# Cross attention: the softmax of the prompt's heads ahead of one weight split on two in-order engines

## The chip, the cores and the metric

The kernel runs on one core of a Trainium2 chip. The metric is the device time of one execution in microseconds; three runs of the kernel before gave 1637.77, 1638.6 and 1644.74, median 1638.6.

## The reference

A two-layer trunk in float32 over 256 prompt tokens and 8 x 4 decoding tokens (288 columns), width 1024. Each layer has a gated feed-forward block, a mixing block (convolution, dilated attention, a linear recurrence), a cross attention, and a second feed-forward block. What the change touches is the cross attention. The prompt's keys and values come from a memory of 256 tokens, the decoding tokens' from caches:

```python
def cross_attend(h, mk, mv, w_q, w_o):
    B, T, D = h.shape
    q = (h @ w_q).reshape(B, T, XATTN_HEADS, XATTN_HEAD_DIM)
    s = jnp.einsum('bthd,bmhd->bhtm', q, mk).astype(F32) * (XATTN_HEAD_DIM ** -0.5)
    p = jax.nn.softmax(s, axis=-1).astype(mv.dtype)
    o = jnp.einsum('bhtm,bmhd->bthd', p, mv).reshape(B, T, D)
    return o @ w_o
...
        if prompt:
            hm = rmsnorm(mem, P['mem_norm'][l])
            mk, mv = jnp.split(hm @ P['xattn_w_kv'][l], 2, axis=-1)
...
        else:
            mk, mv = mem_k_cache[l], mem_v_cache[l]
        x = x + cross_attend(h, mk, mv, P['xattn_w_q'][l], P['xattn_w_o'][l])
```

There are 4 heads of 256, so the prompt has 4 heads x 2 tiles of 128 queries: 8 score tiles of 128 x 256.

## The kernel before

Each engine runs one list of instructions written out by hand, in order; semaphores hold an instruction until others are done. Nothing is scheduled by a program, so an instruction that waits holds all that stand behind it on its engine.

Weights come from HBM as slabs of 1 MB (128 x 2048 floats) into four slots in turn, all asked for by SP in the fixed list `ORDER`; SP asks for slab n once the slot's former holder, slab n - 4, has been read. A weight slab is used as two units of 128 x 1024. Every unit is split for a product in three passes: ScalarE casts it to a high half (`split` in the ScalarE list, line 1508, `w_hi<-slots`), VectorE subtracts to get the low half (`split` in the VectorE list, line 2072, `w_lo<-slots,w_hi`), and TensorE multiplies high by high, high by low and low by high (lines 723 to 725). Three pairs of halves are held at a time, so unit u + 3 is split when TensorE is done with unit u: `next_unit(u)` names the unit that follows u in its place.

In the cross attention TensorE works in this order: value block 0 (before the queries), the 8 column tiles of the queries, the prompt's 8 score tiles against the memory's keys (line 1419), the decoding queries' scores against the cached keys of batches 0 and 1 (line 1406, slabs `memk`), then value block 1, scores 2, value block 2, scores 3, value block 3, and scores 4 to 7. After that come the turns of the probabilities (line 1434) and the products with the values (lines 1445 and 1462). Value block n is 48 matmuls in a pair of PSUM banks and uses value units 2n and 2n + 1, the two halves of slab `kv` 4 + n. Block 1 uses banks 5 and 6, block 2 banks 7 and 5, block 3 banks 0 and 1. So block 2 waits until ScalarE has copied block 1 out of bank 5 (`values_out`, a copy by line 1508, `arena<-bank`).

The "row of the queries" in the change is the loop that, per query tile t, splits the unit that follows it. The last of them, `split(next_unit(UNITS["q"] + 7))`, is value unit 4, the first half of slab `kv` 6. That slab goes into the slot of `memk` 0, so SP asks for it after the decoding scores 0.

The softmax of a prompt's head stands on two engines. VectorE: `row_max(hd)`, a reduction over two score tiles and a scaling (lines 2606, 2608), later `weigh(hd)`, the reciprocal of the sums and a product (lines 2614, 2616). ScalarE between them: `xexp(u)`, one exponential per score tile with its sum (line 1949). The clear of `pz` (line 2620) prepares the decoding side's probabilities. Tile 8 (`xexp(8)`, `row_max(4)`, `weigh(4)`) is the decoding queries' own.

Of the kernel before, what the change touches and what calls it, by code (L numbers as in the profile page):

```python
# [20 lines left out]
KT = D_MODEL // P  # L21
# [33 lines left out]
K_SLABS, V_EARLY = 4, 1  # L55
# [45 lines left out]
UNITS, NUNIT, UNIT_OF_SLAB = {}, 0, {}  # L101
# [7 lines left out]
def value_unit(i):  # L109
    return UNIT_OF_SLAB[SLAB_AT["kv", K_SLABS + i // 2]] + i % 2  # L110
# [146 lines left out]
def program(nc, x_in, mem_in, stream, small, consts, conv_hist, wkv_in, copies, outs, known=None):  # L257
    (y_out, conv_out, kv_out, shift_out, wkv_p_out, wkv_s_out, memk_out, memv_out) = outs
    known = known or {}
    with ExitStack() as ctx:  # L260
# [200 lines left out]
        def bt(ap):  # L461
            return ap.rearrange("p (b t) -> p b t", t=DEC_SEQ)
# [184 lines left out]
        def raw_unit(u):  # L647
            n, half = SLAB_OF_UNIT[u]
            return slots[:, n % NSLOT, half * UNIT:(half + 1) * UNIT]

        def next_unit(u):

            if EXTRA - NW <= u <= EXTRA:
                return u + NW + 1 if u < EXTRA else None
            return u + NW if all(not u < end <= u + NW for end in RUN_ENDS) else None
# [8 lines left out]
        def w_halves(l, u):  # L664
            if u == EXTRA:
                return w_more
            return w_hi[:, w_slot(l, u), :], w_lo[:, w_slot(l, u), :]
# [9 lines left out]
        def unit_head(u):  # L677

            return u // 2
# [821 lines left out]
        def _(act):  # L1501
# [41 lines left out]
            for l in range(DEPTH):  # L1543
                SL.begin_layer()

                def split(u):

                    if u is None:
                        return
                    act.wait_ge(*landed(l, SLAB_OF_UNIT[u][0]))  # L1550
                    if u >= NW and u != EXTRA:
                        act.wait_ge(tensor_done, TL.value(l, ("unit", unit_before(u))))
                    elif l and u < NW:
                        act.wait_ge(tensor_done, TL.value(l - 1, ("unit", NUNIT + u - NW)))
                    copy(w_halves(l, u)[0], raw_unit(u), ("hi", u))
# [86 lines left out]
                t = IN_SEQ[0]  # L1642
# [290 lines left out]
                def values_out(n):  # L1933
                    for mt in range(2):
                        m = 2 * n + mt
                        act.wait_ge(tensor_done, TL.value(l, ("vx", m)))
                        copy(vx[:, mt, n * 256:(n + 1) * 256], bank[V_BANKS[m]][:, 0:256], ("vx", m))

                for n in range(V_EARLY):
                    split(next_unit(value_unit(2 * n)))  # L1940
                    values_out(n)
                    split(next_unit(value_unit(2 * n + 1)))
                for t in range(KT):
                    split(next_unit(UNITS["q"] + t))

                def xexp(u):
                    src = bank[u // 2][:, (u % 2) * MEM:(u % 2 + 1) * MEM] if u < 8 else bank[u - 4][:, 0:MEM]
                    act.wait_ge(vector_done, VL.value(l, ("xnmax", unit_head(u))))
                    SL.done(fn(px[:, u, :], src, ACT.Exp, scale=X_SCALE, bias=xstat[:, 1, u:u + 1],
                               accum_out=xstat[:, 2, u:u + 1]), ("xexp", u))  # L1950

                for u in range(3):
                    xexp(u)
                for n in range(V_EARLY, 4):
                    split(next_unit(value_unit(2 * n)))
                    if n == V_EARLY:
                        xexp(3)
                        xexp(4)
                    values_out(n)
                    split(next_unit(value_unit(2 * n + 1)))  # L1960
                    if n == V_EARLY:
                        xexp(5)
                    if n == V_EARLY + 1:
                        xexp(6)
                        xexp(7)
                xexp(8)

                def probs_T(u):
# [54 lines left out]
        def _(dve):  # L2023
# [33 lines left out]
            for l in range(DEPTH):  # L2057
                VL.begin_layer()

                def settle():  # L2060

                    dve.wait_ge(vector_done, VL.so_far(l))
# [7 lines left out]
                def low(out, src, hi, name=None):  # L2070

                    D(tt(out, src, hi.bitcast(F32), ALU.subtract), name)  # L2072

                def split(u):

                    if u is not None:
                        dve.wait_ge(scalar_done, SL.value(l, ("hi", u)))
                        hi, lo_ = w_halves(l, u)
                        low(lo_, raw_unit(u), hi, ("lo", u))
# [131 lines left out]
                t = IN_SEQ[0]  # L2211
# [77 lines left out]
                for n in range(RAW, IN_TILES):  # L2289
                    t = IN_SEQ[n]  # L2290
# [297 lines left out]
                for t in range(KT):  # L2588
                    dve.wait_ge(tensor_done, TL.value(l, ("q", "cols", t)))
                    if t == 0:  # L2590
                        settle()
                    D(tt(qx[:, t, :], bank[t % 7][:, 0:T], rs[:], ALU.mult))
                    if t == 0:
                        dve.wait_ge(pool_done, PL.value(l, "qz_clear"))
                    D(tt(qz_own[:, t], bt(bank[t % 7][:, TP:T]), bt(rs[:, TP:T]), ALU.mult), ("qx", t))
                    split(next_unit(UNITS["q"] + t))
                def two_units(hd):

                    if hd < 4:
                        return bank[hd][:, :].rearrange("p (q m) -> p q m", q=2), slice(2 * hd, 2 * hd + 2)  # L2600
                    return bank[4][:, 0:MEM].unsqueeze(1), slice(8, 9)

                def row_max(hd):
                    src, u = two_units(hd)
                    dve.wait_ge(tensor_done, TL.value(l, ("xs", u.stop - 1)))
                    D(nc.vector.tensor_reduce(xstat[:, 0, u], src, AX_X, ALU.max))
                    settle()
                    D(ts(xstat[:, 1, u], xstat[:, 0, u], -X_SCALE, None, ALU.mult), ("xnmax", hd))

                def weigh(hd):  # L2610
                    src, u = two_units(hd)
                    n = u.stop - u.start
                    dve.wait_ge(scalar_done, SL.value(l, ("xexp", u.stop - 1)))
                    D(nc.vector.reciprocal(xstat[:, 3, u], xstat[:, 2, u]))
                    settle()
                    D(tt(px[:, u, :], px[:, u, :], xstat[:, 3, u].unsqueeze(2).to_broadcast([P, n, MEM]), ALU.mult), ("xprobs", hd))

                row_max(0)
                dve.wait_ge(tensor_done, TL.value(l, ("xs", 7)))
                D(nc.vector.memset(pz, 0.0), "pz_clear")  # L2620
                row_max(1)
                weigh(0)
                for n in range(V_EARLY, 4):
                    if n < 3:
                        row_max(n + 1)
                    split(next_unit(value_unit(2 * n)))
                    weigh(n)
                    split(next_unit(value_unit(2 * n + 1)))
                row_max(4)
                weigh(4)  # L2630
# [178 lines left out]
```

## Time and profile before

| | |
|---|---|
| profiled execution | 1638.07 us, span 1636.3 us |
| TensorE matmuls busy | 1573.7 us, 96% of the span |
| VectorE / ScalarE / GpSimd busy | 1045.0 / 729.5 / 242.3 us |
| chain that ended last, by engine | PE 79%, DVE 9%, ACT 5%, DMA 5%, issue 2% |
| splits: ScalarE casts `w_hi` x374, VectorE `w_lo` x370 | 388.4 us at 1046 ns; 462.7 us at 1253 ns |
| exponentials of the cross attention (line 1949) | 18, of 474 ns in the median |
| mean granted TensorE clock | 0.991 |

Busy times of the engines overlap. A share of the chain says which engine the end of the program depended on, stretch by stretch. The granted clock is given as a share of 2.4 GHz. Engines are named PE (TensorE), PEld (its weight loads), DVE (VectorE), ACT (ScalarE), POOL (GpSimd) and SP in the rows; L12 is line 12 of the kernel before. The two layers run the same list, some 806 us apart.

### The profile page before, as it was taken

To read this page: it belongs to the slowest core of one execution; us is meant where nothing else is said; L and a number is where in the kernel's file an instruction comes from. 1 tells how busy PE (TensorE), PEld (TensorE's weight loads), DVE (VectorE), ACT (ScalarE), POOL (GpSimd) and SP (SyncE) were. 2 spreads that over 40 slices of the span, in tenths; PEclk is the share of its full clock that TensorE was granted. 3 is DMA by queue.
4 is the path that set the end of the run, shared out by engine and by line. 5 is a ranking of instruction groups with operands and counts; after the bars stand their busy time and mean duration, and the time that the engine had idled before them with its cause. 6 is when DMAs were issued, how large, how long until landed. Compare 5 with 4: busy or idle time off the path is not lost.

```text
span 1636.3 us, 31568 instructions
## 1 busy us (share of the span) xinstructions
PE 1573.7 (96%) x13436; PEld 1487.3 (91%) x13436; DVE 1045.0 (64%) x1628; ACT 729.5 (45%) x1235; POOL 242.3 (15%) x223
## 2 busy tenths in 40 slices
PE   8999999899999899999999999998999989999997
PEld 8999998897799689999999999998868977999997
DVE  6787556977554367675477764679773642777744
ACT  5445357534352354343354444573333523544433
POOL 1010000893020010000010000029800200100000
PEclk9999999999999999999999999999999999999999
DMA  6764544302547766755355544442136477666550
GB/s 236 292 223 164 198 143 146 132 29 87 205 162 289 311 247 246 282 183 173 130 188 216 183 166 161 136 152 94 35 128 255 173 288 281 236 256 263 176 177 33
DMA packets 40269, 305.75 MB, mean 187 GB/s; under 512 B 4865, under 2 KB 5025, under 8 KB 7457
## 3 DMA queue, kind: packets, MB, share of 16 engines
q1 hardware_dynamic: 37504, 288.88, 48.4%
q0 software_dynamic: 2048, 11.17, 1.9%
q10 hardware_dynamic: 576, 3.67, 0.6%
q8 instruction: 107, 1.75, 0.4%
q14 instruction: 34, 0.27, 0.0%
HBM read 292.90 MB, written 37.88 MB: 202 GB/s over the span
## 4 chain that ended last, share of the span: by engine, by line
PE 79%; DVE 9%; ACT 5%; DMA 5%; issue 2%; DVEq 0%; ACTq 0%
PE bank L723 20%; PE bank L725 20%; PE bank L724 20%; DMA slots<-stream 5%; PE bank L1019 3%; PE bank L919 3%; DVE w_lo L2072 2%; ACT w_hi L1508 2%; PE bank L1462 1%; PE bank L1419 1%; PE bank L1445 1%; PE bank L1335 1%; ACT arena L1508 1%; PE bank L883 1%; PE bank L842 1%
## 5 line engine op out<-in xcount | busy, mean ns | idle before, releaser
L2072 DVE TENSOR_TENSOR w_lo<-slots,w_hi 128x1024 fp32r<-128x1024 f32 x370 | 462.7, 1253 | 348.0 <-ACT w_hi L1508 346.3
L723 PE MATMUL bank<-h_hi,w_hi 128*128 128x288 f32 x1808 | 540.7, 299 | 11.9 <-DVE w_lo L2072 5.0
L1508 ACT CAST w_hi<-slots 128x1024 fp32r<-128x1024 f32 x374 | 388.4, 1046 | 358.4 <-PE bank L725 271.7
L724 PE MATMUL bank<-h_lo,w_hi 128*128 128x288 f32 x1808 | 534.7, 296 | 0.0
L725 PE MATMUL bank<-h_hi,w_lo 128*128 128x288 f32 x1808 | 532.9, 295 | 0.0
L723 PEld LDWEIGHTS bank<-h_hi,w_hi 128*128 128x128 f32 x1808 | 340.0, 188 | 18.5 <-DVE w_lo L2072 7.2
L725 PEld LDWEIGHTS bank<-h_hi,w_lo 128*128 128x128 f32 x1808 | 341.8, 189 | 0.0
L724 PEld LDWEIGHTS bank<-h_lo,w_hi 128*128 128x128 f32 x1808 | 340.8, 188 | 0.4
L725 PE MATMUL bank<-hid_hi,w_lo 128*128 128x288 f32 x704 | 207.7, 295 | 0.0
L724 PE MATMUL bank<-hid_lo,w_hi 128*128 128x288 f32 x704 | 207.3, 294 | 0.0
L723 PE MATMUL bank<-hid_hi,w_hi 128*128 128x288 f32 x704 | 207.1, 294 | 0.0
L1508 ACT COPY arena<-bank 128x256 f32<-128x256 f32 (+7 forms) x224 | 76.8, 379 | 205.1 <-PE bank L725 59.0
L554 POOL TENSOR_TENSOR arena<-arena 128x288 f32<-128x288 f32 (+1 forms) x52 | 49.4, 950 | 739.3 <-ACT arena L1558 735.9
L725 PEld LDWEIGHTS bank<-hid_hi,w_lo 128*128 128x128 f32 x704 | 132.1, 188 | 0.0
L723 PEld LDWEIGHTS bank<-hid_hi,w_hi 128*128 128x128 f32 x704 | 132.1, 188 | 0.0
L724 PEld LDWEIGHTS bank<-hid_lo,w_hi 128*128 128x128 f32 x704 | 132.0, 188 | 0.0
L1592 ACT ACTIVATE arena<-arena 128x288 f32<-128x288 f32 x88 | 39.2, 446 | 166.4 <-DVE arena L2111 166.4
L589 POOL TENSOR_SCALAR arena<-arena,par_all 128x256 f32<-128x256 f32 x88 | 100.3, 1150 | 3.9
L1019 PE MATMUL bank<-arena,slots 128*128 128x256 f32 x256 | 65.0, 390 | 2.5 <-ACT arena L1508 2.1
L919 PE MATMUL bank<-arena 64*64 64x64 f32 x1488 | 55.0, 226 | 9.2 <-DVE arena L2354 7.2
L919 PEld LDWEIGHTS bank<-arena 64*64 64x64 f32 x1488 | 52.4, 141 | 11.7 <-DVE arena L2354 7.7
L605 POOL TENSOR_TENSOR arena<-arena 128x512 f32<-128x512 f32 x44 | 61.1, 1388 | 0.3
(348 smaller groups left out, 2160.2 us busy)
## 6 DMA issues: line engine op xcount, KB each, us to landing
slots<-stream SPq DMA_DIRECT2D x235, 1024.0 KB, 5.0
out_win3k<-win3k SPq DMA_DIRECT2D x2, 4080.0 KB
out_win3v<-win3v SPq DMA_DIRECT2D x2, 4080.0 KB
arena<-stream SPq DMA_DIRECT2D x4, 1024.0 KB, 8.7
h_mem<-stream SPq DMA_DIRECT2D x4, 1024.0 KB, 6.0
out_win2k<-win2k SPq DMA_DIRECT2D x2, 2032.0 KB
out_win2v<-win2v SPq DMA_DIRECT2D x2, 2032.0 KB
con<-consts SPq DMA_DIRECT2D x1, 2308.0 KB, 10.6
```

What stands on the lines that cost most here:

```text
L554: PL.done(nc.gpsimd.tensor_tensor(squares[:, 0, :], squares[:, 0, :], squares[:, k, :], ALU.add), (tag, "added", k))
L589: p_ = nc.gpsimd.tensor_scalar(out, up[:, ch, tap:tap + TP], w, None, ALU.mult)
L605: PL.done(nc.gpsimd.tensor_tensor(ycv[:, :, 0:TP], ycv[:, :, 0:TP], prod[:, tap % 2, :, 0:TP], ALU.add), ("summed", tap))
L723: mm(out, lhs[0], rhs[0], start=start, stop=False)
L724: mm(out, lhs[0], rhs[1], start=False, stop=False)
L725: return mm(out, lhs[1], rhs[0], start=False, stop=stop)
L842: i = mm(bank[b][:, 0:T], lora[rows, off + j * P:off + (j + 1) * P], src, start=True, stop=True)
L919: i = mm(bank[b][o_, s_], lhs[r_, s_], rhs[r_, s_], start=True, stop=True)
L1019: i = mm(bank[b][:, 0:MEM], w[:, t % 2, k, :], hm[:, k, :], start=k == 0, stop=k == KT - 1)
L1508: return SL.done(nc.scalar.copy(out, in_), name)
L1592: SL.done(fn(th[:, t % 2, :], gs[:, t % 2, :], ACT.Tanh, scale=0.5), (tag, "tanh", t))
L2072: D(tt(out, src, hi.bitcast(F32), ALU.subtract), name)
```

## The change

On ScalarE all eight exponentials of the prompt's heads stand directly behind the split that precedes the last one of the queries' row, and the last one behind them; before, three stood behind it and five among the splits and copies of value blocks 1 and 2. On VectorE the four row maxima, the four weighings and the clear of `pz` stand ahead of that last split as well; before they stood behind it and among the following splits.

```diff
@@ -1940,7 +1940,7 @@
                     split(next_unit(value_unit(2 * n)))
                     values_out(n)
                     split(next_unit(value_unit(2 * n + 1)))
-                for t in range(KT):
+                for t in range(KT - 1):
                     split(next_unit(UNITS["q"] + t))
 
                 def xexp(u):
@@ -1949,20 +1949,13 @@
                     SL.done(fn(px[:, u, :], src, ACT.Exp, scale=X_SCALE, bias=xstat[:, 1, u:u + 1],
                                accum_out=xstat[:, 2, u:u + 1]), ("xexp", u))
 
-                for u in range(3):
+                for u in range(8):
                     xexp(u)
+                split(next_unit(UNITS["q"] + KT - 1))
                 for n in range(V_EARLY, 4):
                     split(next_unit(value_unit(2 * n)))
-                    if n == V_EARLY:
-                        xexp(3)
-                        xexp(4)
                     values_out(n)
                     split(next_unit(value_unit(2 * n + 1)))
-                    if n == V_EARLY:
-                        xexp(5)
-                    if n == V_EARLY + 1:
-                        xexp(6)
-                        xexp(7)
                 xexp(8)
 
                 def probs_T(u):
@@ -2593,7 +2586,8 @@
                     if t == 0:
                         dve.wait_ge(pool_done, PL.value(l, "qz_clear"))
                     D(tt(qz_own[:, t], bt(bank[t % 7][:, TP:T]), bt(rs[:, TP:T]), ALU.mult), ("qx", t))
-                    split(next_unit(UNITS["q"] + t))
+                    if t < KT - 1:
+                        split(next_unit(UNITS["q"] + t))
                 def two_units(hd):
 
                     if hd < 4:
@@ -2615,16 +2609,16 @@
                     settle()
                     D(tt(px[:, u, :], px[:, u, :], xstat[:, 3, u].unsqueeze(2).to_broadcast([P, n, MEM]), ALU.mult), ("xprobs", hd))
 
-                row_max(0)
+                for hd in range(4):
+                    row_max(hd)
+                    if hd:
+                        weigh(hd - 1)
                 dve.wait_ge(tensor_done, TL.value(l, ("xs", 7)))
                 D(nc.vector.memset(pz, 0.0), "pz_clear")
-                row_max(1)
-                weigh(0)
+                weigh(3)
+                split(next_unit(UNITS["q"] + KT - 1))
                 for n in range(V_EARLY, 4):
-                    if n < 3:
-                        row_max(n + 1)
                     split(next_unit(value_unit(2 * n)))
-                    weigh(n)
                     split(next_unit(value_unit(2 * n + 1)))
                 row_max(4)
                 weigh(4)
```

On ScalarE, behind the queries' splits (`CAST w_hi`; `ACTIVATE` of line 1949 are the exponentials, `COPY` takes a value block out of PSUM), lines with - are of before and with + of the change:

```order
-L1508 CAST w_hi<-slots 128x1024 x9
+L1508 CAST w_hi<-slots 128x1024 x8
 L1949 ACT_TABLE_LOAD
-L1949 ACTIVATE arena<-bank,arena 128x256 x3
-L1508 CAST w_hi<-slots 128x1024
-L1949 ACTIVATE arena<-bank,arena 128x256 x2
+L1949 ACTIVATE arena<-bank,arena 128x256 x8
+L1508 CAST w_hi<-slots 128x1024 x2
 L1508 COPY arena<-bank 128x256 x2
```

Value unit 4's cast is the last of the nine; it moved behind the exponentials, and unit 5's cast follows it at once, with the two copies of value block 1 directly behind.

On VectorE at the same place, before (the first row is the low half of value unit 4, the last that of value unit 5):

```order
L2072 TENSOR_TENSOR w_lo<-slots,w_hi 128x1024
L2606 TENSOR_REDUCE arena<-bank 128x2
L2608 TENSOR_SCALAR arena<-arena 128x2
L2620 MEMSET arena 128x2112
L2606 TENSOR_REDUCE arena<-bank 128x2
L2608 TENSOR_SCALAR arena<-arena 128x2
L2614 RECIPROCAL arena<-arena 128x2
L2616 TENSOR_TENSOR arena<-arena 128x512
L2606 TENSOR_REDUCE arena<-bank 128x2
L2608 TENSOR_SCALAR arena<-arena 128x2
L2072 TENSOR_TENSOR w_lo<-slots,w_hi 128x1024
```

And there in the change, from the weighing of head 1 on (its line numbers are 6 or 7 lower, the clear's 3):

```order
L2608 RECIPROCAL arena<-arena 128x2
L2610 TENSOR_TENSOR arena<-arena 128x512
L2600 TENSOR_REDUCE arena<-bank 128x2
L2602 TENSOR_SCALAR arena<-arena 128x2
L2608 RECIPROCAL arena<-arena 128x2
L2610 TENSOR_TENSOR arena<-arena 128x512
L2617 MEMSET arena 128x2112
L2608 RECIPROCAL arena<-arena 128x2
L2610 TENSOR_TENSOR arena<-arena 128x512
L2065 TENSOR_TENSOR w_lo<-slots,w_hi 128x1024 x4
```

All row maxima and weighings of the prompt and the clear now stand ahead of the low half of value unit 4, and the four low halves of units 4 to 7 follow one another.

## Rows read from the trace of the kernel before

**Rows 1.** TensorE's waits, 485 to 600: who for whom, total us, times, longest

```profile
PE bank L723 <- ACT arena L1508: 5.9, 1, 5.9
```

**Rows 2.** Timeline of TensorE, layer 0: start us, length us, instruction, [idle before <- releaser]

```profile
517.76 7.14 PE L1419 MATMUL bank<-arena 128*128 128x256 f32 x32 [0.69 <-issue]
...
532.64 1.07 PE L1406 MATMUL bank<-slots,arena 128*32 128x256 f32 x16
539.62 0.55 PE L723 MATMUL bank<-w_hi,hm_hi 128*128 128x256 f32 x1 [5.92 <-ACT arena L1508]
...
547.64 1.07 PE L1406 MATMUL bank<-slots,arena 128*32 128x256 f32 x16
548.64 0.39 PE L723 MATMUL bank<-w_hi,hm_hi 128*128 128x256 f32 x1
...
554.58 3.66 PE L1406 MATMUL bank<-slots,arena 128*32 128x256 f32 x64
```

**Rows 3.** Timeline of TensorE, layer 1, the same places

```profile
1339.19 1.07 PE L1406 MATMUL bank<-slots,arena 128*32 128x256 f32 x16
1346.12 0.55 PE L723 MATMUL bank<-w_hi,hm_hi 128*128 128x256 f32 x1 [5.86 <-ACT arena L1508]
...
1353.70 1.07 PE L1406 MATMUL bank<-slots,arena 128*32 128x256 f32 x16
```

**Rows 4.** The chain that ended last, layer 0: start us, length us, what

```profile
525.96 4.75 DMA slots<-stream
530.74 1.06 ACT w_hi L1508
531.83 1.23 DVE w_lo L2072
...
539.26 0.27 ACT arena L1508
```

**Rows 5.** Timeline of ScalarE, layer 0

```profile
530.74 1.05 ACT L1508 CAST w_hi<-slots 128x1024 fp32r<-128x1024 f32 x1 [15.74 <-DMA slots<-stream]
```

**Rows 6.** Windows: stretch, its us, busy us by engine, PEclk, DMA share, GB/s

```profile
536.00:539.00 3.00, 0.00 (x0) 0.00 (x0) 2.90 (x8) 2.16 (x6) 0.00 (x0) 0.76 1.03 434
539.00:542.00 3.00, 2.38 (x11) 2.41 (x12) 2.59 (x5) 2.21 (x7) 0.00 (x0) 0.50 0.76 229
...
545.00:548.00 3.00, 3.00 (x31) 2.78 (x33) 1.68 (x3) 1.68 (x3) 0.00 (x0) 1.00 0.01 3
```

**Rows 7.** Line 1949, whole program: ns min/median/max, first and last start

```profile
L1949 ACT ACTIVATE arena<-bank,arena x18: 464/474/509, 533.9 to 1365.4; 128x256 f32<-128x256 f32 x18
L1949 ACT ACT_TABLE_LOAD  x2: 1283/1283/1283, 531.8 to 1338.3; - x2
```

**Rows 8.** Timeline of VectorE, layer 0

```profile
534.24 1.82 DVE L2620 MEMSET arena<- 128x2112 f32 x1 [0.38 <-issue]
535.97 0.63 DVE L2606 TENSOR_REDUCE arena<-bank 128x2 f32<-128x512 f32 x1
...
537.52 0.68 DVE L2606 TENSOR_REDUCE arena<-bank 128x2 f32<-128x512 f32 x1
...
549.27 0.69 DVE L2616 TENSOR_TENSOR arena<-arena 128x512 f32<-128x512 f32 x1
```

**Rows 9.** SP's requests, layer 1 (memk 3 and kv 7; memk 4; memk 6 and 7), us to landing

```profile
L514 SPq DMA_DIRECT2D slots<-stream x2: 328/379/430, 1333.4 to 1333.8; - x2
DMA to landing us min/median/max: 7.5/8.6/9.7
...
L514 SPq DMA_DIRECT2D slots<-stream x1: 328/328/328, 1340.3 to 1340.3; - x1
DMA to landing us min/median/max: 8.1/8.1/8.1
...
L514 SPq DMA_DIRECT2D slots<-stream x2: 328/380/432, 1354.8 to 1355.2; - x2
DMA to landing us min/median/max: 4.8/6.5/8.3
```

## The prediction, made before the changed kernel ran

> **What bounds the kernel now.** I read the shares of the chain that ended last first (in the table above): TensorE holds 79% of it, so a change pays only where TensorE stands still. Next came the list of what TensorE waits for around the first layer's cross attention. It has one large entry: 5.9 us, once, for a ScalarE result [rows 1]. The timeline of TensorE puts that wait at 539.62, before the first matmul of value block 2, right behind the decoding queries' scores against memk 2 [rows 2]. Layer 1 shows the same: 5.86 us at 1346.12 [rows 3].
>
> Then I read the chain of waits backwards from 539.62 [rows 4]. The matmul waited for a PSUM copy on ScalarE, the copy of value block 1 out of bank 5, which block 2 writes again. That copy stood behind two casts and five exponentials on ScalarE, those behind row maxima and a clear of `pz` on VectorE, and at the head of it all is a DMA: slab kv 6 was asked for at 525.96 and its cast began at 530.74. The cast is the last split of the queries' row (value unit 4, half of kv 6). ScalarE stood idle 15.74 us before it [rows 5], and since an engine runs its instructions in order, the eight exponentials behind it stood there too. The scores they read come out of TensorE from 517.76, a head every 1.8 us, and all are there at 517.76 + 7.14 = 524.90 [rows 2]. So some ten microseconds of softmax that could run in idle time run after the slab's arrival, ahead of a PSUM copy that TensorE needs.
>
> The wait has a second price. The granted clock is 1.00 until TensorE stops, 0.76 on average in 536 to 539, 0.50 in 539 to 542 with the matmuls running again, and 1.00 in 545 to 548 [rows 6]: the 1.2 GHz level after the standstill, 2.4 GHz before and later. Value block 2 therefore took 547.64 - 539.62 = 8.02 us, block 3, with the same instructions, 554.58 - 548.64 = 5.94 [rows 2]; in layer 1 block 2 took 1353.70 - 1346.12 = 7.58 [rows 3].
>
> **The change part by part.** TensorE, SP and POOL keep their rows, no instruction is added, none removed. Four things move.
>
> *The exponentials go ahead of the cast.* The table load of 1.28 us [rows 7] waits for nothing and falls into the idle 15.74 us. A row maximum and a weighing together take 537.52 - 535.97 = 1.55 us of VectorE [rows 8], two exponentials about 1 us of ScalarE (0.47 us each, and a short read of the sum) [rows 7]. Heads come every 1.8 us, so the softmax keeps pace with the scores, and behind the last score there remain the last row maximum and one weighing (1.55), the weighing of head 2, which may be late (0.8), and the clear (1.82 [rows 8]): 524.9 + 4.2 = about 529.1 on VectorE, and on ScalarE about 527.5. Both are done before 530.74, when the cast can begin, and 531.83, when VectorE is wanted. Cost: nothing. The cover is that idle stretch; without it the 4.2 us behind the last score would lie in front of the split, which is the bound above. The bound below is nothing too, since the cast cannot begin before the slab is there.
>
> *The cast of value unit 4 stays where the DMA puts it.* Slab kv 6 goes into a slot that the scores against memk 0 free; TensorE reaches these at the same time as before. Cast at 530.74, its low half done at 531.83 + 1.23 = 533.06 [rows 4].
>
> *The cast of value unit 5 and the two copies follow directly.* Unit 5 is the other half of the same slab. ScalarE: 530.74 + 1.06 + 1.05 = 532.85, then the copy of bank 5 (0.27), done at about 533.2 instead of 539.53 [rows 4].
>
> *TensorE.* The scores against memk 2 begin at 532.64 and last 548.64 - 547.64 = 1.00 (the same step one block later) [rows 2], so block 2 may begin at 533.64. Its weights are there at 533.06, its bank at 533.2: no wait is left. At full clock it ends at 533.64 + 5.94 = 539.58 instead of 547.64: 8.06 us earlier. Layer 1: 1339.19 + 1.00 + 5.94 = 1346.13 instead of 1353.70: 7.57 us [rows 3]. Together 15.63, of which 11.8 are the two waits and about 3.8 the low clock after them.
>
> On that second part the Trainium skill, page "TensorE: Matmul & The Clock Gate", section "What's actually happening", says that the length of the slow stretch varies from run to run and should not be fitted. The two layers here differ in the same way: 2.08 and 1.64 us were lost on the same work. By the page the gain could be anything from the 11.8 of the waits upwards; by the rows it is 15.6.
>
> *What is late next.* Value block 3 needs slab kv 7, the last scores need memk 7. I take layer 1, where landings were later. Memk 3 and kv 7 were asked for at 1333.4 and 1333.8 and took 7.5 and 9.7, so they landed at 1340.9 and 1343.5: one slab each 2.6 us when they queue [rows 9]. Cast and low half of value unit 6 take 1.05 and 1.23, so it is ready at 1345.8, and TensorE wants it at 1346.13 + 1.00 = 1347.13: 1.3 us to spare. Memk 4 lands at 1340.3 + 8.1 = 1348.4 [rows 9]; memk 5, asked for earlier than now, follows at 1351.0, memk 6 (its slot is freed at 1347.1) at 1353.6, memk 7 at 1356.2. TensorE wants it three quarters into the last scores: 1347.13 + 5.94 + 2.75 = 1355.8 (2.75 of the 3.66 in rows 2). So about 0.4 us of waiting there. Now it lands at 1355.2 + 8.3 = 1363.5 [rows 9] while TensorE, by the same sum from 1353.70, comes to it at 1353.70 + 1.00 + 5.94 + 2.75 = 1363.4: as tight as that already. Bounds: nothing (it does not wait in layer 0), and 2.6, a whole slab's time; I take 0.4, which is the sum of landings. Layer 0 lands its slabs earlier in the block and gets no such term.
>
> Behind it all, transfers of memv and of the output weights are asked for by events of TensorE, and move with it; its other waits there are small and stay.
>
> Sum: 1638.07 - 8.06 - 7.57 + 0.4 = 1622.8 for an execution like the profiled one (span 1636.3 and 1.8 around it). The median of the three runs, 1638.6, lies 0.5 above it, so 1623.3.
>
> **The rivals.**
>
> *Transfers take it back.* VectorE frees the slot of kv 6 some 5 us earlier, so memk 5 is asked for while kv 7, memv 3 and memk 4 are still on their way. If all shared the engines instead of following each other, none need land before the last of them: 1348.4 + 2.6 = 1351.0 in layer 1. Value unit 6 would be ready at 1353.3, TensorE would wait 6.2 us for it and pay about 1.9 of low clock: 8.1 of the 7.6 gained. Both layers: about 1638, no change. For it: the DMA share is full in this stretch (1.03 in 536 to 539 [rows 6]). Against it: slabs asked for within 0.4 us of each other landed 2.6 apart, in order [rows 9]. The Trainium skill, page "DMA: Bandwidth & Descriptors", section "Two DMAs through the same engine are not ordered", says that nothing orders transfers across the 16 DMA engines, which is the rule behind this rival; the rows contradict it only as far as two slabs go.
>
> *The waits go but the clock does not come back.* Were the low clock tied to something other than the standstill (it also falls with ScalarE and VectorE busy), only 5.92 + 5.86 = 11.8 would be won: 1627.2 with the other terms. Against it: block 3 runs at 1.00 with both engines at work [rows 2, 6].
>
> *The softmax becomes the bound.* Now it takes from 533.06 to 549.27 + 0.69 = 549.96 [rows 4, 8], 16.9 us, with its waits. If it took that long from the last scores on as well, it would end at 541.8, the low half of unit 4 at 543.0, and block 2 would begin 3.4 us later than today: 1638.6 + 6.8 = 1645.4, slower. It decides from the point where the softmax needs more than 13.5 us behind 524.9 (539.62 less the split's 1.23). Against it: the instructions sum to a third of that, the rest are casts and waits for TensorE that no longer stand between.
>
> **How the numbers follow.** Forecast as summed, 0.83; only the waits, 0.06; transfers, 0.08; softmax, 0.03. The forecast by itself reaches from 1622.4, which is without the term for memk 7, less the 2 us by which a low-clock stretch can differ (2.08 was paid in one), so 1620, up to a whole slab's time in each layer: 1623.3 + 2 x 2.6 - 0.4 = 1628.1. That takes in the second case; of the third the range takes only the edge: 1620 to 1629.5. A measurement of this kernel tells some 0.5%, 8.2 us, from no change, so faster means under 1630.4: the first two cases and a little of the third, 0.90; within it 0.07; slower 0.03.
>
> **What would show it.** In the profile after: exponentials from about 520.5, the table load by 517, ScalarE's cast of kv 6 still near 530.7; no entry of 5.9 us in TensorE's waits; value blocks 2 and 3 about 5.9 us long each at clock 1.00; TensorE at the last scores near 546.5. A wait before block 3 would speak for the transfers; exponentials that end behind 531 for the softmax. A TensorE wait of more than 4 us anywhere between 533 and 570 would make the prediction wrong.

## The result and the profile after

The changed kernel took 1625.62 us in the median (1623.55 to 1633.39, 7 runs), the kernel before 1640.21 on the same chips (1636.64 to 1644.74, 7 runs): ratio 0.9923, 95% interval 0.9898 to 0.9948, so between 8.5 and 16.7 us faster. A second set gave 0.9924 (0.9906 to 0.9941). Forecast: 1623.3, range 1620 to 1629.5.

TensorE's waits from 485 to 600 (for whom, total us, times, longest) no longer hold the entry of [rows 1]:

```profile
PE bank L723 <- DVE w_lo L2065: 2.1, 5, 0.7
PE bank L1434 <- ACT arena L1508: 1.8, 2, 1.0
PE bank L1406 <- DMA slots<-stream: 1.0, 1, 1.0
PE bank L1419 <- issue: 0.7, 1, 0.7
```

The third line is new: a wait for a slab. TensorE's timeline of the changed kernel in layer 0, from the prompt's scores to the first output column, shows where it is:

```profile
519.61 7.14 PE L1419 MATMUL bank<-arena 128*128 128x256 f32 x32 [0.70 <-issue]
...
534.49 1.07 PE L1406 MATMUL bank<-slots,arena 128*32 128x256 f32 x16
535.49 0.39 PE L723 MATMUL bank<-w_hi,hm_hi 128*128 128x256 f32 x1
...
541.42 1.07 PE L1406 MATMUL bank<-slots,arena 128*32 128x256 f32 x16
542.42 0.39 PE L723 MATMUL bank<-w_hi,hm_hi 128*128 128x256 f32 x1
...
548.37 2.80 PE L1406 MATMUL bank<-slots,arena 128*32 128x256 f32 x48
552.18 1.07 PE L1406 MATMUL bank<-slots,arena 128*32 128x256 f32 x16 [1.01 <-DMA slots<-stream]
...
572.81 0.37 PE L723 MATMUL bank<-ox_hi,w_hi 128*128 128x288 f32 x1
```

Value block 2 starts 1.00 behind scores 2, without a wait, and takes 541.42 - 535.49 = 5.93 us, as block 3 does (5.95). In [rows 2] it waited 5.92 and took 8.02. Then the last scores wait 1.01 for slab memk 7. In layer 1 block 2 starts without a wait as well, and the same slab is waited for:

```profile
1350.08 1.07 PE L1406 MATMUL bank<-slots,arena 128*32 128x256 f32 x16 [0.72 <-DMA slots<-stream]
```

The granted clock in layer 0 (in the row behind the busy times: clock, DMA share, GB/s) stays up:

```profile
535.00:537.00 2.00, 2.00 (x24) 1.59 (x17) 1.25 (x2) 0.34 (x2) 0.00 (x0) 1.00 1.04 434
539.00:541.00 2.00, 2.00 (x19) 2.00 (x19) 1.96 (x2) 1.33 (x3) 0.00 (x0) 1.00 0.97 401
```

ScalarE's timeline, layer 0, the answer to [rows 5]:

```profile
515.80 1.05 ACT L1508 CAST w_hi<-slots 128x1024 fp32r<-128x1024 f32 x1 [2.15 <-PE bank L725]
516.87 1.28 ACT L1949 ACT_TABLE_LOAD   x1
522.54 0.47 ACT L1949 ACTIVATE arena<-bank,arena 128x256 f32<-128x256 f32 x1 [4.39 <-DVE arena L2602]
...
527.72 0.47 ACT L1949 ACTIVATE arena<-bank,arena 128x256 f32<-128x256 f32 x1 [0.70 <-DVE arena L2602]
...
532.81 2.00 ACT L1508 CAST w_hi<-slots 128x1024 fp32r<-128x1024 f32 x2 [4.07 <-DMA slots<-stream]
534.71 0.64 ACT L1508 COPY arena<-bank 128x256 f32<-128x256 f32 x2
```

The idle 15.74 us in front of slab kv 6 have shrunk to 4.07, because table load and exponentials run in them. The slab's cast begins 13.2 us behind the first score (532.81 - 519.61), as good as in the kernel before (530.74 - 517.76 = 13.0), and both casts and the copies out of banks 5 and 6 follow at once. VectorE, the answer to [rows 8]:

```profile
528.86 1.82 DVE L2617 MEMSET arena<- 128x2112 f32 x1 [0.39 <-PE bank L1406]
530.60 0.11 DVE L2608 RECIPROCAL arena<-arena 128x2 f32<-128x2 f32 x1
530.74 0.69 DVE L2610 TENSOR_TENSOR arena<-arena 128x512 f32<-128x512 f32 x1
533.89 2.36 DVE L2065 TENSOR_TENSOR w_lo<-slots,w_hi 128x1024 fp32r<-128x1024 f32 x2 [2.45 <-ACT w_hi L1508]
```

It is done with the softmax at 531.43 and waits 2.45 us for the cast: the cover that the prediction counted on is there, and 2.45 us of it are left on VectorE.

The unit for what follows is the stretch from the first of the prompt's score matmuls to the first output column on TensorE: before, 60.04 us in layer 0 and 59.89 in layer 1; after, 53.20 (572.81 - 519.61) and 53.14. Together the stretches are 13.6 us shorter, while the profiled spans differ by 12.5 (1636.3 to 1623.8); the rest of the program was 1.1 longer. In the ten profiled executions of this document that rest (span less both stretches) lies between 1515.4 and 1523.5, whatever the kernel, and neither lowest nor highest belongs to the kernel before (1516.4). Totals cannot tell 2 us. The stretches can: two profiles of the changed kernel differ by 0.28 and 0.46 us in them.

### The profile page after: what moved, and what is told of

The parts are those of the page before. It is cut to its first block, busy times and chain, and to the rows that moved or that the text cites. A ratio compares the mean times of both kernels' runs of the same rounds, so it can differ in the third digit from the quotient of the medians.

```text
span 1623.8 us, 31568 instructions
## 1 busy us (share of the span) xinstructions
PE 1572.3 (97%) x13436; PEld 1485.1 (91%) x13436; DVE 1043.7 (64%) x1628; ACT 728.9 (45%) x1235; POOL 242.6 (15%) x223
## 4 chain that ended last, share of the span: by engine, by line
PE 80%; DVE 8%; DMA 6%; ACT 5%; issue 1%; SPq 0%; DVEq 0%; ACTq 0%
PE bank L723 20%; PE bank L725 20%; PE bank L724 20%; DMA slots<-stream 5%; PE bank L1019 4%; PE bank L919 3%; DVE w_lo L2065 3%; ACT w_hi L1508 2%; PE bank L1419 1%; PE bank L1274 1%; PE bank L1335 1%; ACT arena L1508 1%; PE bank L883 1%; DMA arena<-mem_in 1%; PE bank L1406 1%
```

## The experiments

Stretches in us, totals as ratio to the kernel before on the same chip:

| kernel | layer 0 | layer 1 | ratio (95%) |
|---|---|---|---|
| before | 60.04 | 59.89 | 1 |
| changed | 53.20 | 53.14 | 0.9923 (0.9898 to 0.9948) |
| changed, again | 52.92 | 52.68 | 0.9924 (0.9906 to 0.9941) |
| before, filler on TensorE | 57.98 | 58.50 | 0.9986 (0.9968 to 1.0003) |
| before, copies first | 53.22 | 54.22 | 0.9920 (0.9888 to 0.9952) |
| changed, two clears more | 53.83 | 54.03 | one run only |
| changed, five clears more | 63.08 | 62.41 | 1.0044 (1.0022 to 1.0066) |
| changed, scores 3 earlier | 52.23 | 52.21 | 0.9918 (0.9894 to 0.9943) |
| the same, again | 52.28 | 52.35 | 0.9899 (0.9884 to 0.9913) |
| the same and early turns | 51.58 | 51.77 | 0.9910 (0.9897 to 0.9924) |

**The clock's part alone.** On the kernel before:

```diff
                     sample_scores(n + 1)
+                    if n == V_EARLY:
+                        for _ in range(12):
+                            mm(bank[7][:, 0:256], ident, con[:, 0:256], start=True, stop=True)
```

> The kernel before, with twelve matmuls of 128x256 that nobody reads (5.35 us, from 7.14 us for 16 of their kind) put on TensorE between the decoding scores 2 and value block 2, where it stood still for 5.9 us. Nothing is moved on ScalarE or VectorE. Theory (the standstill lowers the clock, and block 2 pays for it): block 2 starts near 539.6 as before but takes 5.9 us instead of 8.0 and 7.6, granted clock 1.00 throughout, stretch from the prompt's scores to the output columns 2.1 and 1.6 us shorter, total about -3.7 us. Rival (the low clock belongs to the busy stretch of ScalarE and VectorE): block 2 stays at 8.0 us and 0.50, total unchanged.

TensorE, layer 0: the filler begins at 537.50, block 2 at 543.54, scores 3 at 549.44.

```profile
536.50 1.07 PE L1406 MATMUL bank<-slots,arena 128*32 128x256 f32 x16
537.50 0.70 PE L1429 MATMUL bank<-con 128*128 128x256 f32 x2
...
543.54 0.35 PE L723 MATMUL bank<-w_hi,hm_hi 128*128 128x256 f32 x1 [0.59 <-ACT arena L1511]
...
549.44 1.07 PE L1406 MATMUL bank<-slots,arena 128*32 128x256 f32 x16
```

```profile
542.00:545.00 3.00, 2.41 (x17) 1.99 (x16) 2.55 (x6) 3.00 (x10) 0.00 (x0) 1.00 0.89 289
```

ScalarE's copy comes no earlier: block 2 starts 21.92 us into the stretch, in the kernel before 21.86. But it takes 5.90 us at clock 1.00, with VectorE and ScalarE as busy as before. The stretches are 2.06 and 1.39 us shorter, 3.45 together where 3.7 was expected. In layer 1 block 2 took 5.92 us instead of 7.58, but slab kv 6, and with it the copy, came 0.6 us later into the stretch than in the kernel before. So the slow block belongs to the standstill. The total moved the same way, but its interval includes 1.

**Is it the early softmax, or only the copy?** On the kernel before, the softmax stays behind the split:

```diff
-                for u in range(3):
+                split(next_unit(value_unit(2)))
+                values_out(1)
+                for u in range(5):
                     xexp(u)
...
+                split(next_unit(value_unit(3)))
+                xexp(5)
+                split(next_unit(value_unit(4)))
+                values_out(2)
+                xexp(6)
+                xexp(7)
+                values_out(3)
...
+                split(next_unit(value_unit(2)))
                 row_max(0)
-                dve.wait_ge(tensor_done, TL.value(l, ("xs", 7)))
-                D(nc.vector.memset(pz, 0.0), "pz_clear")
                 row_max(1)
                 weigh(0)
...
+                row_max(2)
+                weigh(1)
+                split(next_unit(value_unit(3)))
+                row_max(3)
+                split(next_unit(value_unit(4)))
+                weigh(2)
+                dve.wait_ge(tensor_done, TL.value(l, ("xs", 7)))
+                D(nc.vector.memset(pz, 0.0), "pz_clear")
+                weigh(3)
```

> The kernel before, with the softmax left behind the last split of the queries' row, but behind the split of value unit 5 and the two copies of value block 1 as well; the clear of pz goes behind the later splits. Theory (what counts is only the copy out of bank 5 and the two splits, not that the softmax is early): block 2 starts directly behind the decoding scores 2, as in the changed kernel, and the total is that of the changed kernel within 2 us (about -13). Rival (the softmax must be out of the way early, or it delays the splits of block 3 and the turned probabilities): TensorE waits 2 us or more per layer before block 3 or behind the last scores, total half the gain or less.

```profile
534.10 1.07 PE L1406 MATMUL bank<-slots,arena 128*32 128x256 f32 x16
535.10 0.39 PE L723 MATMUL bank<-w_hi,hm_hi 128*128 128x256 f32 x1
...
542.39 0.36 PE L723 MATMUL bank<-w_hi,hm_hi 128*128 128x256 f32 x1 [0.28 <-ACT w_hi L1508]
...
551.81 1.07 PE L1406 MATMUL bank<-slots,arena 128*32 128x256 f32 x16 [0.71 <-DMA slots<-stream]
```

Block 2 starts just as early as in the changed kernel, and layer 0 has the changed kernel's stretch to 0.02 us. Layer 1 waits 1.83 for memk 7, the wait that the changed kernel has there too (0.72). The softmax then costs 0.28 and 0.16 us before block 3. It also delays the low half of value unit 7, and with it the request of memk 7, which goes into the slot of kv 7: 25.0 and 24.9 us into the stretch (544.2 and 1349.2), in the changed kernel 23.3. In layer 0 memk 7 landed 0.1 us later, in layer 1 1.4, and that layer's stretch is 1.1 longer than the changed kernel's. So up to 1.1 us of one layer may hang on the softmax being early; the rest of the gain is had without it. Most of what the change brought, then, is that ScalarE's copy and the splits no longer stand behind the softmax; that the softmax is early is one way to it.

**How much cover there is.** On the changed kernel, five or two clears of `pz` more:

```diff
                 dve.wait_ge(tensor_done, TL.value(l, ("xs", 7)))
+                for _ in range(5):
+                    D(nc.vector.memset(pz, 0.0))
+                    settle()
                 D(nc.vector.memset(pz, 0.0), "pz_clear")
```

> The changed kernel, with the clear of pz done five times more, on VectorE, ahead of the last split of the queries' row (5 x 1.82 = 9.1 us; nothing else is changed). Theory (the softmax costs nothing only as long as it ends before the slab): VectorE has 2.5 us to spare, so the low half of value unit 4 comes 6.6 us later, at about 541.8 on the changed kernel's clock of time, 6.2 us behind the point where TensorE wants it; the clock falls again, block 2 takes about 8 us, the loss is 8 us a layer and the total is back at about 1638 to 1641. Rival (the order alone brought the gain): the loss is small, under 4 us.

TensorE, layer 0, and the clock in two windows:

```profile
535.93 1.07 PE L1406 MATMUL bank<-slots,arena 128*32 128x256 f32 x16
545.78 0.55 PE L723 MATMUL bank<-w_hi,hm_hi 128*128 128x256 f32 x1 [8.79 <-DVE w_lo L2065]
553.98 1.07 PE L1406 MATMUL bank<-slots,arena 128*32 128x256 f32 x16
```

```profile
545.00:548.00 3.00, 2.21 (x10) 2.25 (x11) 2.91 (x3) 0.00 (x0) 0.00 (x0) 0.50 0.09 16
548.00:551.00 3.00, 3.00 (x16) 3.00 (x15) 0.00 (x0) 0.00 (x0) 0.00 (x0) 0.51 0.91 339
```

The mechanism is the expected one: TensorE waits for the low half of unit 4, the clock falls to its lower level, block 2 takes 8.20 us. The size was off: each clear took 2.32 us up to the next one's start, not 1.82, so 11.6 us were added and the wait was 8.79 instead of 6.2. The loss is 9.9 and 9.3 us a layer where 8 were expected, and the kernel became slower than the one before: this is what the third rival of the prediction would have looked like.

> The changed kernel with the clear of pz done twice more ahead of the last split (2 x 2.32 us as the clears with their waits took in the run with five). Theory: five clears, 11.6 us, gave a wait of 8.8 us, so 2.8 us are free; two give a wait of 1.8 us before value block 2 in each layer. If the low clock needs a long standstill, block 2 still takes 5.9 us at clock 1.00, and the stretch grows by 1.8 us less what the last scores then wait less (up to 1.0), 0.8 to 1.8 us a layer. Rival: any wait costs clock, block 2 takes 7 us or more.

```profile
535.15 1.07 PE L1406 MATMUL bank<-slots,arena 128*32 128x256 f32 x16
538.03 0.35 PE L723 MATMUL bank<-w_hi,hm_hi 128*128 128x256 f32 x1 [1.81 <-DVE w_lo L2065]
...
543.94 1.07 PE L1406 MATMUL bank<-slots,arena 128*32 128x256 f32 x16
```

The wait is 1.81, as worked out from the run with five, and block 2 takes 5.91 us, at clock 1.00 from 538 to 544: a standstill of 1.8 us cost no clock, those of 5.9 and 8.8 did. The stretch grew by only 0.63 and 0.89 us over the first profile of the changed kernel (0.91 and 1.35 over the second), because TensorE came later to the last scores and no longer waited for memk 7 there.

**The new wait.** On the changed kernel:

```diff
+                        if n == 2 and half == 0:
+                            sample_scores(3)
...
-                    sample_scores(n + 1)
+                    if n != 2:
+                        sample_scores(n + 1)
```

> The changed kernel, with the decoding scores against memk 3 between the two halves of value block 2 instead of behind it, so that the slot for memk 6 is free about 3 us earlier. Theory (memk 7 is late because memk 6 and 7 are asked for too late): the waits for a slab before the last scores, 1.0 and 0.7 us, fall to 0.3 or less each, total about -1.2 us against the changed kernel. Rival (the transfer queue is full there, and a slab asked for earlier lands no earlier): the waits stay.

```profile
537.87 1.07 PE L1408 MATMUL bank<-slots,arena 128*32 128x256 f32 x16
538.87 0.39 PE L723 MATMUL bank<-w_hi,hm_hi 128*128 128x256 f32 x1
...
547.69 3.92 PE L1408 MATMUL bank<-slots,arena 128*32 128x256 f32 x64
551.54 0.66 PE L1437 MATMUL bank<-con,arena 128*128 128x128 f32 x4
```

The last scores run through in 3.85 us, where the changed kernel took 4.81 (548.37 to 553.18, the turns' start). The stretches are 0.97 and 0.93 shorter than in the first profile of the changed kernel, 0.69 and 0.47 than in the second. The request of memk 6 in layer 0:

```profile
L514 SPq DMA_DIRECT2D slots<-stream x1: 328/328/328, 539.0 to 539.0; - x1
DMA to landing us min/median/max: 9.0/9.0/9.0
```

That is 20.1 us into the stretch and landed at 29.1; in the changed kernel it was asked for at 23.0 and landed at 30.0. So the theory holds, and the rival in part: of 2.9 us by which the slab was asked for earlier, 0.9 came out at its landing.

> The changed kernel with the decoding scores against memk 3 inside value block 2, once more. Theory: the stretch is 0.95 us shorter per layer than in the changed kernel, so 1.9 us in total, if the rest of the program keeps its time. Rival: the time saved is waited for elsewhere, and the total is that of the changed kernel.

Again 52.28 and 52.35. Against the changed kernel's second profile, taken beside it, that is only 0.64 and 0.33 us shorter where 0.95 a layer was expected: that profile waited less for memk 7 (0.58 and 0.50), and 0.17 us of waiting was left in layer 1 here. The total was 1623.58 us, ratio 0.9899, against 1627.62 for the changed kernel, and their intervals overlap:

> The changed kernel once more, on the same chip as the next ones, for the total. Theory: about 13 us below the kernel before (0.992).

**Using the early softmax.** On this last kernel, the copies of the turned probabilities stand ahead of `xexp(8)` on ScalarE, and on TensorE:

```diff
-                for u in range(4):
-                    probs_T(u)
+                for b_ in range(MEMK_EARLY, DEC_BATCH):
+                    probs_T(2 * (b_ - MEMK_EARLY)) if b_ < DEC_BATCH - 1 else None
+                    probs_T(2 * (b_ - MEMK_EARLY) + 1) if b_ < DEC_BATCH - 1 else None
+                    sample_scores(b_)
```

> The changed kernel with the decoding scores against memk 3 between the halves of value block 2, and with the turns of the first two heads' probabilities among the last decoding scores (two in front of scores 5, two in front of scores 6) and their copies on ScalarE ahead of the decoding queries' exponential. This is possible only because the softmax is done early. Theory: nothing else is in the way there, so the wait of 1.0 us between the turns goes, the last scores lose their 1.0 and 0.7 us, and the stretch from the prompt's scores to the output columns falls from 53.2 and 53.1 us to about 51.2 in each layer, 4 us less in total than the changed kernel. Rival: the turned copies only push the decoding exponential later, and the wait comes back before its turn; the stretch stays at the 52.2 of the kernel with the moved scores alone.

```profile
549.38 1.07 PE L1408 MATMUL bank<-slots,arena 128*32 128x256 f32 x16
550.38 0.66 PE L1435 MATMUL bank<-con,arena 128*128 128x128 f32 x4
550.97 1.07 PE L1408 MATMUL bank<-slots,arena 128*32 128x256 f32 x16
551.97 0.66 PE L1435 MATMUL bank<-con,arena 128*128 128x128 f32 x4
552.55 1.93 PE L1408 MATMUL bank<-slots,arena 128*32 128x256 f32 x32
```

The turns run between the scores without a wait. The stretches are the shortest of all, 51.6 and 51.8, half of the further gain expected: 0.16 us of waiting is left in front of the decoding queries' turn and 0.58 in front of the third head's. Over the changed kernel that is 0.9 to 1.6 us a layer. The total (1624.32 in the median, ratio 0.9910) does not tell it from the kernel before it in this list.

## Why the prediction was right

*The two waits.* Worked out as gone; gone in both layers. The slab's arrival, the two casts, the copy and the start of block 2 came at the places in the stretch that the sum gave them, within 0.3 us.

*The clock.* 3.8 us worked out from block 2 against block 3. The filler gave 3.45 back without an earlier copy, and the rival by which the clock belonged to the other engines' work falls with it. The Trainium skill, page "TensorE: Matmul & The Clock Gate", section "HAM oscillation — how this bites in real kernels", says that a long enough wait between groups of matmuls lets the clock drop, so that the next group starts slow. These runs agree: block 2 lost 1.3 to 2.3 us after waits of 5.9 to 8.8 us, nothing after 1.8.

*The softmax's cover.* Predicted done at about 529.1 on VectorE; it was 531.43 - 1.85 = 529.6 (the changed kernel's stretch began 1.85 later). Two more clears used up the cover and showed its edge.

*Transfers.* Value unit 6 was in time in both layers, so the rival in which earlier requests hold up kv 7 did not happen. What failed is the sizing of the step "what is late next": 0.4 us of waiting for memk 7, in layer 1 alone, "Layer 0 lands its slabs earlier in the block and gets no such term". Measured were 1.01 and 0.72 (0.58 and 0.50 in the second profile). The requests of memk 5, and of memk 6 and 7, in layer 0 of the changed kernel (start, then us to landing):

```profile
L514 SPq DMA_DIRECT2D slots<-stream x1: 328/328/328, 536.3 to 536.3; - x1
DMA to landing us min/median/max: 9.9/9.9/9.9
```

```profile
L514 SPq DMA_DIRECT2D slots<-stream x2: 328/380/433, 542.6 to 542.9; - x2
DMA to landing us min/median/max: 7.0/8.1/9.2
```

Memk 5 landed at 546.2, memk 6 at 549.6, memk 7 at 552.1. The sum had taken 2.6 us a slab throughout; memk 6 came 3.4 behind memk 5 (2.9 in layer 1). Asked for earlier, with scores 3 moved, it came 2.5 behind it. The sum put memk 7 at 31.9 us into layer 1's stretch (1356.2 - 1324.31); it came at 32.2 there and 32.5 in layer 0, where TensorE wanted it at 31.6. Kv 6 to memk 7 now follow one another without the pause of [rows 6]. In layer 0 kv 7 still landed 1.2 us earlier into the stretch than in layer 1 (18.3 for 19.5), but by memk 6 that lead was gone (30.0 for 29.9); why is not shown.

*The sum.* 15.2 us were expected from the stretches, 13.6 and 14.3 measured in the two profiles; most of the 1.6 missing in the first is the slab wait (1.73 for 0.4). With scores 3 earlier, where that wait is all but gone, 15.5 and 15.3 come out, close to the 15.63 of the sum without it. The total, 1625.62 for 1623.3, says less: the rest of the program alone varies by 8 us, so that it lies so near is in part luck. The forecast also stood on a median of 1638.6 from three runs, where seven gave 1640.21. A slip in the range changes nothing: its lower end starts from 1622.4, the sum without memk 7 but also without the 0.5 us up to the median; it should have started from 1622.9.

## What to carry to other kernels

On an engine that works in order, look for an instruction that waits for a transfer and has ready work behind it: the work is free if it goes ahead, as long as its inputs are there early and it ends before the transfer does; the most room there can be is the idle time in front of the waiting instruction. If it does not fit, ask whether what the bottleneck waits for can go ahead of that work instead, as the run with the copies first shows. Count the slow matmuls behind a long standstill as part of its price, by comparing the block after it with an equal one later. When a stall goes, the requests that it used to spread out become one queue, so ask of each slab in it when it lands and when it is wanted, in every repetition and not only in the worst.

## What was not expected of the hardware

```profile
532.63 1.82 DVE L2618 MEMSET arena<- 128x2112 f32 x1 [0.51 <-DVE arena L2618]
```

In the run with five clears more, clears of the same tile, each waiting for the last, took 2.32 us apiece for 1.82 of work: 0.51 us lie between the end of one and the start of the next. It is not the wait for VectorE's own semaphore alone: the scaling behind each row maximum waits for it in the same way and started 0.03 us behind the reduction in the changed kernel (522.33, behind 521.61 + 0.69). And in the kernel before, the clear started 0.38 us late with nothing to wait for that the profile shows [rows 8]. Why a clear starts late is not shown.
